# The up product of an MLP as seven half-size block products per unit

## The chip, the cores and the metric

One core of a Trainium2 chip runs two transformer blocks in float32 as one program. The metric is the device time in microseconds; less is better. TensorE (PE) multiplies into PSUM banks, VectorE (DVE) and ScalarE (ACT) prepare operands and take results, GpSimd (POOL) and SyncE (SP) issue transfers.

## The reference, cut to what matters

The first block (gated mixing, a recurrent branch, a mixture of experts) and the attention part of the second are the same in both kernels. Changed is the MLP at the end: x is 512 x 1024, w_ff1 1024 x 4096 and w_ff2 4096 x 1024, all float32.

```python
def rms_norm(x, g):
    xf = x.astype(jnp.float32)
    y = xf * lax.rsqrt(jnp.mean(xf * xf, axis=-1, keepdims=True) + EPS)
    return (y * g.astype(jnp.float32)).astype(x.dtype)
...
        h2 = rms_norm(x, norm_mlp[layer])
        x = x + jnp.square(jax.nn.relu(h2 @ w_ff1[layer])) @ w_ff2[layer]
    return rms_norm(x, norm_final)
```

## The kernel before

Every large float32 product is made of three fp32r products. An operand is split in two: ACT copies it to fp32r (the high part), DVE subtracts that from the original (the low part), and PE multiplies high by high, high by low and low by high into one bank. The activations h2, transposed to features by tokens (8 tiles of 128 features, 512 tokens), lie in `act_hi` and `act_lo`. The norm's scale is applied when results are added to `x`, so the row squares (`mlp_squares`, ACT) may be late.

The hidden width 4096 is worked in two halves, and each half is an up product followed by a down product. **An up product** has 4 units of 512 hidden columns; a unit has two chunks of 512 input rows, and a chunk four tiles of 12 matmuls, 128 weight columns by 512 tokens. Chunks alternate between the pairs `w_hi`/`w_lo` 0 and 1. SP loads chunk c into `w_stage[c % 2]` (1 MB) once chunk c - 2 has its low part; ACT may write chunk c's high part once PE has finished chunk c - 2; so a load has about two chunks of time. ACT takes each bank with a ReLU, DVE squares it into `hidden`.

**A down product** is already seven half-size block products (parts 0 to 6) of a 512 x 2048 by 2048 x 1024 product: each part has two steps of 24 matmuls, 512 columns wide, 14 steps in all. Part n's A operand (a quarter of `hidden` or a sum of quarters, `sum_three`, `sum_two`, `sum_one`, `sum_four`) goes to `part_hi`/`part_lo`, a step's weight block to `w_hi`/`w_lo`; `step_stage` names the buffer of each step. Sums of weight blocks are not made by DVE: ACT negates a loaded block (`negate`), and POOL issues transfers that add another block to it in SBUF (`add_block`, number k of 1 to 5 for each of kc = 0, 1, in that program order; each waits for the one before it on the same block column). Steps 4 and 5 need two adds, steps 8 and 9 the third (`b_one[1]`, `b_far`), steps 6 and 7 the fourth (`w_stage`), steps 12 and 13 the fifth. In the kernel before, `b_sum` is negated behind unit 1 of a half and `b_one[1]` and `b_far` behind its unit 2.

Nothing plans the order: each engine runs its own list as written (`two_blocks` has one section per engine), and semaphores tie them together. An instruction that waits holds all that stands behind it on its engine. The lists that matter are SP's at L820 to L850, POOL's at L1011 to L1030, ACT's at L1605 to L1705, DVE's at L2600 to L2705 and PE's at L3500 to L3536. The pieces that repeat (the low part on DVE, an adding transfer on POOL):

```python
    def rest(dst, src, hi):
        return dve.tensor_tensor(dst, src, hi.bitcast(F32), ALU.subtract)
...
    def add_block(h, kc, k, dst, block):
        pool.wait_ge(b_added[kc], loaded(h, "added", k - 1))
        pool.dma_start(dst[:, :, :], block, accum_op=ALU.add).then_inc(b_added[kc], 16)
```

## Time and profile before

| | us |
|---|---|
| median of 3 runs | 1690.91 |
| lowest and highest | 1690.90, 1691.43 |
| the profiled execution | 1689.05 |
| its span, first to last instruction | 1687.4 |
| up product, second half | 87.25 |
| a down product | 76.2 |

The profile comes from one execution. PE is busy for 99% of the span, but the busy time of matmuls overlaps, so times of stages are read from starts. A row of a timeline gives start and duration and, in brackets, how long the engine was idle before it and what released it.

### The profile page before, as it was taken

To read this page: it belongs to the slowest core of one execution; us is meant where nothing else is said; L and a number is where in the kernel's file an instruction comes from. 1 tells how busy PE (TensorE), PEld (TensorE's weight loads), DVE (VectorE), ACT (ScalarE), POOL (GpSimd) and SP (SyncE) were. 2 spreads that over 40 slices of the span, in tenths; PEclk is the share of its full clock that TensorE was granted. 3 is DMA by queue.
4 is the path that set the end of the run, shared out by engine and by line. 5 is a ranking of instruction groups with operands and counts; after the bars stand their busy time and mean duration, and the time that the engine had idled before them with its cause. 6 is when DMAs were issued, how large, how long until landed. Compare 5 with 4: busy or idle time off the path is not lost.

```text
span 1687.4 us, 23046 instructions
## 1 busy us (share of the span) xinstructions
PE 1672.0 (99%) x9378; PEld 1217.1 (72%) x9378; DVE 896.4 (53%) x1217; ACT 618.6 (37%) x744; POOL 112.8 (7%) x168
## 2 busy tenths in 40 slices
PE   9999999999999999999999999999999999999998
PEld 7888888865454535454588877788888888888886
DVE  6425438452343334324668755567675544773487
ACT  6334433321111101111366633344642245652565
POOL 4000000000000000000011012210000001100100
PEclk9999999999999999999999999999999999999999
DMA  7332222948999999999541332124352358756974
GB/s 274 100 99 75 75 75 101 354 189 342 429 428 428 428 429 429 428 429 428 204 153 53 100 100 75 51 76 132 107 188 100 107 181 195 157 149 221 200 157 128
DMA packets 90703, 353.29 MB, mean 209 GB/s; under 512 B 7856, under 2 KB 7872, under 8 KB 78208
## 3 DMA queue, kind: packets, MB, share of 16 engines
q1 hardware_dynamic: 78288, 325.95, 50.4%
q0 software_dynamic: 12336, 26.23, 7.8%
q8 instruction: 56, 0.92, 0.2%
q14 instruction: 23, 0.19, 0.0%
HBM read 345.87 MB, written 6.29 MB: 209 GB/s over the span
## 4 chain that ended last, share of the span: by engine, by line
PE 97%; DMA 1%; DVE 1%; ACT 0%; issue 0%; POOL 0%; DVEq 0%; POOLq 0%; ACTq 0%
PE bank L2764 51%; PE bank L3117 12%; PE bank L3522 9%; PE bank L3130 7%; PE bank L3025 4%; PE bank L3065 3%; PE bank L3297 2%; PE bank L2789 2%; PE bank L2810 1%; DMA ring<-in_w 1%; PE bank L3327 1%; PE bank L3350 1%; PE bank L3397 1%; PE bank L3222 1%; PE bank L3430 0%; PE bank L3436 0%
## 5 line engine op out<-in xcount | busy, mean ns | idle before, releaser
L2764 PE MATMUL bank<-act_hi,w_hi 128*128 128x512 f32 x992 | 390.0, 393 | 0.0
L2764 PE MATMUL bank<-act_hi,w_lo 128*128 128x512 f32 x992 | 386.2, 389 | 0.0
L2764 PE MATMUL bank<-act_lo,w_hi 128*128 128x512 f32 x992 | 386.2, 389 | 0.0
L1754 DVE TENSOR_TENSOR w_lo<-w_stage,w_hi 128x2048 fp32r<-128x2048 f32 x79 | 181.1, 2293 | 208.9 <-ACT w_hi L1044 208.8
L1044 ACT ACTIVATE w_hi<-w_stage 128x2048 fp32r<-128x2048 f32 x79 | 151.4, 1917 | 242.0 <-PE bank L2764 223.7
L3117 PE MATMUL bank<-ring,xgT 128*64 128x512 f32 x992 | 216.1, 592 | 1.8 <-ACT xgT L1266 1.4
L2764 PEld LDWEIGHTS bank<-act_hi,w_hi 128*128 128x128 f32 x992 | 186.2, 188 | 40.8 <-issue 2.9
L2764 PEld LDWEIGHTS bank<-act_hi,w_lo 128*128 128x128 f32 x992 | 186.2, 188 | 39.1
L2764 PEld LDWEIGHTS bank<-act_lo,w_hi 128*128 128x128 f32 x992 | 186.3, 188 | 37.7
L3117 PEld LDWEIGHTS bank<-ring,xgT 128*64 128x64 f32 x992 | 71.0, 137 | 143.0 <-issue 139.5
L3130 PE MATMUL bank<-ring,gatedT 128*64 128x512 f32 x512 | 113.4, 595 | 3.1 <-DMA ring<-in_w 2.3
L1294 ACT ACTIVATE y_hi_sb<-bank,slot_tables 128x512 fp32r<-128x512 f32 x32 | 22.0, 687 | 224.7 <-PE bank L3130 223.4
L2143 DVE TENSOR_TENSOR gated<-gated,bank 128x512 f32<-128x512 f32 x16 | 11.0, 688 | 161.7 <-PE bank L3117 161.7
L3130 PEld LDWEIGHTS bank<-ring,gatedT 128*64 128x64 f32 x512 | 35.8, 137 | 72.4 <-issue 68.7
L3522 PE MATMUL bank<-w_hi,part_hi 128*128 128x512 f32 x224 | 87.1, 389 | 0.0
L3522 PE MATMUL bank<-w_lo,part_hi 128*128 128x512 f32 x224 | 87.1, 389 | 0.0
L3522 PE MATMUL bank<-w_hi,part_lo 128*128 128x512 f32 x224 | 87.1, 389 | 0.0
L2118 DVE TENSOR_TENSOR x_tm<-x_tm,bank 128x512 f32<-128x512 f32 x128 | 78.5, 681 | 0.3 <-PE bank L3065 0.3
L2764 PE MATMUL bank<-w_hi,act_hi 128*128 128x512 f32 x160 | 62.8, 393 | 0.0
L2764 PE MATMUL bank<-w_hi,act_lo 128*128 128x512 f32 x160 | 62.3, 390 | 0.0
L2764 PE MATMUL bank<-w_lo,act_hi 128*128 128x512 f32 x160 | 62.3, 389 | 0.0
L2159 DVE SCALAR_TENSOR_TENSOR y_lo_sb<-bank,slot_tables,y_hi_sb 128x512 fp32r<-128x512 f32 x32 | 23.2, 749 | 73.4 <-ACT y_hi_sb L1294 73.1
(490 smaller groups left out, 2366.6 us busy)
## 6 DMA issues: line engine op xcount, KB each, us to landing
ring<-in_w SPq DMA_DIRECT2D x94, 2048.0 KB, 16.8
w_stage<-in_w_in SPq DMA_DIRECT2D x42, 1024.0 KB, 5.1
w_stage<-in_w_ff SPq DMA_DIRECT2D x24, 1024.0 KB, 5.6
b_sum<-in_w_ff POOLq DMA_DIRECT2D x12, 1024.0 KB, 12.7
w_stage<-in_w_out SPq DMA_DIRECT2D x8, 1024.0 KB, 5.0
b_one<-in_w_ff SPq DMA_DIRECT2D x6, 1024.0 KB, 7.7
branch_gates<-gate_out POOLq DMA_DIRECT2D x16, 256.0 KB, 2.5
w_stage<-in_w_proj_gla SPq DMA_DIRECT2D x4, 1024.0 KB, 9.9
```

What stands on the lines that cost most here:

```text
L1044: act.activation(w_hi[s][:, 0:ktiles, :], w_stage[s][:, 0:ktiles, :], ACT.Copy)\
L1754: dve.tensor_tensor(w_lo[s][:, 0:ktiles, :], w_stage[s][:, 0:ktiles, :], w_hi[s][:, 0:ktiles, :].bitcast(F32), ALU.subtract).then_inc(w_lo ...
L2118: dve.tensor_tensor(xt, xt, bank[:, :], ALU.add).then_inc(moe_added, 1)
L2159: dve.scalar_tensor_tensor(y_lo_sb[:, half], gb[1 + b][:, :], slot_gate[:, col(i)], y_hi_sb[:, half].bitcast(F32), ALU.mult, ALU.subtract)\
L2764: ins = pe.matmul(banks[j][:, :], left, right, start=(kc == 0 and k == 0 and n_pass == 0), stop=(kc == g.chunks - 1 and k == g.ktiles - 1 ...
L2789: return pe.transpose(dst, src, ident[0:rows, 0:rows])
L3025: return pe.matmul(bank[:, (k % 2) * 2 * P:(k % 2 + 1) * 2 * P], part[:, t, k * P:(k + 1) * P], sel[:, t, :], start=start, stop=(part is x ...
L3065: ins = pe.matmul(bank[:, :], selT[:, t * P:(t + 1) * P], part[:, half], start=(part is y_hi_sb), stop=(part is y_lo_sb))
L3117: ins = pe.matmul(dst[mine, :], xgT[:, 4 * kh + k, slots], up_weights(2 * w + kh, q, k, ahead), start=(kh == 0 and k == 0), stop=(kh == 1 ...
L3130: return pe.matmul(gb[1 + nh][mine, :], gatedT[:, k, mine], ring[4 + k // 2][:, 4 * q + 2 * (k % 2) + nh, :], start=(k == 0), stop=(k == 3 ...
L3297: ins = pe.matmul(v_bank[n][j][:, :], left[:, k0 + k, cols], right[:, k, :], start=(part_first[n] and k == 0 and n_pass == 0), stop=(k == ...
L3522: ins = pe.matmul(part_bank[n][j][:, :], left[:, ka, cols], right[:, k, :], start=(part_first[n] and kc == 0 and k == 0 and n_pass == 0), ...
```

## The change

Unit 0 of the up product stays as it was. Units 1 to 7 (`BLOCKED` = 7) become one run ahead of both down products. A unit's product, 512 weight columns by 1024 rows by 512 tokens, is cut in halves in all three, and made of seven products of half-size blocks: a product has 24 matmuls with 128 weight columns as the stationary operand and 256 tokens as the moving one, two groups of 128 hidden columns into the two halves of one bank.

The token side needs four sums T1 to T4 of quarters of h2, made once; for that ACT copies each transposed tile twice, to `raw_T` in plain float32 and to `act_hi`. The weight side needs sums W1 to W4 for each unit, on DVE. The weight blocks' high and low parts go to three slots of half size, so that ACT may write product m's slot when product m - 3 is done. Loads of a unit are now one of 1 MB and two of 0.5 MB with rows of 1 KB. Banks are shared by several products: ACT copies partial sums out, DVE adds, ACT does ReLU and square. All 32 tiles of `hidden` are kept (`F + 0` on, 64 KB a partition), so buffers of the down product move, and `b_one[1]` (now in the space of `act_lo`) and `b_far` are loaded at the end of unit 7 and negated behind step 2's high part. The second down product's first loads, first operands and `b_sum` adds are issued during the first one.

The core of the diff (the order of steps 3 to 13 inside a down product is otherwise as before):

```diff
+    g_up = Gemm(g_out2, 1, 2, "act")
+    BLOCKED = FF // 512 - 1
+    g_blk = Gemm(g_up, BLOCKED, PARTS, "act", tiles=3)
+    sums_added = g_blk.out["dve"]
+    g_blk.out["dve"] += 3 * BLOCKED
+    g_down = []
+    for h in range(HALVES):
+        g_down.append(Gemm(g_down[-1] if h else g_blk, 2, PARTS, "dve", tiles=PARTS))
...
+        slot_page = (41, 45, 37)
+        slot_hi = [at(f"slot_hi{s}", page, [P, 4, 256], F32R) for s, page in enumerate(slot_page)]
+        slot_lo = [at(f"slot_lo{s}", page + 2, [P, 4, 256], F32R) for s, page in enumerate(slot_page)]
+        w11, w21 = w_stage[0][:, :, 0:256], w_stage[0][:, :, 256:512]
+        w12, w22 = w_stage[1][:, :, 0:256], w_stage[1][:, :, 256:512]
+        w_sum = [at(f"w_sum{s}", 8 + 2 * s, [P, 4, 256]) for s in range(2)]
...
+            for u in range(1, BLOCKED + 1):
+                if u == 1:
+                    sp.wait_ge(w_lo_done, split_count(g_up.chunk0))
+                else:
+                    sp.wait_ge(hid_summed, w_summed(u - 1, W3))
+                load_rows(w_stage[0][:, :, :], 0, 512 * u, 512, w_loaded[0])
+                if u == 1:
+                    sp.wait_ge(w_lo_done, split_count(g_up.chunk0 + 1))
+                else:
+                    sp.wait_ge(hid_summed, w_summed(u - 1, W4))
+                load_rows(w12, 1, 512 * u, 256, w_loaded[1])
+                if u > 1:
+                    sp.wait_ge(w_lo_done, blk_split(u - 1, 6))
+                load_rows(w22, 1, 512 * u + 256, 256, far_loaded)
...
+            sp.wait_ge(hid_summed, w_summed(BLOCKED, W3))
+            sp.dma_start(w_stage[0][:, :, :], weight_block(0, 0, 0, 0)).then_inc(w_loaded[0], 16)
+            sp.wait_ge(w_lo_done, blk_split(BLOCKED, 5))
+            sp.wait_ge(pe_tiles, products_done(BLOCKED, 3))
+            sp.dma_start(b_one[1][:, :, :], weight_block(0, 0, 1, 0)).then_inc(b_one_in[1], 16)
+            sp.dma_start(b_far[:, :, :], weight_block(0, 0, 1, 1)).then_inc(b_one_in[0], 16)
+            sp.wait_ge(w_lo_done, blk_split(BLOCKED, 6))
+            sp.dma_start(w_stage[1][:, :, :], weight_block(0, 0, 0, 1)).then_inc(w_loaded[1], 16)
+            for h in range(HALVES):
                 for kc in range(2):
                     sp.wait_ge(w_lo_done, step(h, kc))
...
-                act.activation(act_hi[:, 4 * b:4 * b + 4, t * P:(t + 1) * P],
-                               mb[t][:, :].rearrange("p (k t) -> p k t", k=4), ACT.Copy).then_inc(n_hi, 1)
+                turned = mb[t][:, :].rearrange("p (k t) -> p k t", k=4)
+                act.activation(raw_T[:, 4 * b:4 * b + 4, t * P:(t + 1) * P], turned, ACT.Copy).then_inc(raw_copied, 1)
+                act.activation(act_hi[:, 4 * b:4 * b + 4, t * P:(t + 1) * P], turned, ACT.Copy).then_inc(n_hi, 1)
...
+            def slot_high(u, n):
+                m = product(u, n)
+                act.wait_ge(pe_tiles, 4 * (g_blk.chunk0 + max(m - 2, -1)))
+                if n == 0:
+                    act.wait_ge(w_loaded[0], 16 * (g_up.chunk1 // 2 + u))
+                elif n == 1:
+                    act.wait_ge(w_loaded[1], 16 * (g_up.chunk1 // 2 + u))
+                elif n == 6:
+                    act.wait_ge(far_loaded, 48 + 16 * u)
+                else:
+                    act.wait_ge(hid_summed, w_summed(u, {2: W2, 3: W1, 4: W3, 5: W4}[n]))
+                source = (w11, w12, w_sum[1][:, :, :], w_sum[0][:, :, :], w_sum[0][:, :, :], w_sum[1][:, :, :], w22)[n]
+                act.activation(slot_hi[m % 3][:, :, :], source, ACT.Copy).then_inc(w_hi_done, 1)
...
+            split_hi(g_up.chunk0 + 1, 1)
+            t_high(T2)
+            t_high(T3)
+            for t in range(NT):
+                mlp_squares(t)
+            own.settle()
+            act.sem_inc(n_sd, NT)
+            slot_high(1, 0)
+            slot_high(1, 1)
+            for j in range(4):
+                act.wait_ge(pe_tiles, (g_up.chunk0 + 1) * 4 + j + 1)
+                if j >= 2:
+                    act.wait_ge(hid_sq, j - 1)
+                act.activation(relu_t[j % 2][:, :], gb[j][:, :], ACT.Relu).then_inc(out_act, 1)
+                act.wait_ge(out_act, g_up.tile0 + 4 + j + 1)
+                act.activation(hidden[:, j, :], relu_t[j % 2][:, :], ACT.Square).then_inc(hid_sq, 1)
...
+            for u in range(1, BLOCKED + 1):
+                slot_high(u, 2)
+                if u == 1:
+                    t_high(T1)
+                copy_first(u)
+                slot_high(u, 3)
+                if u > 1:
+                    relu_sum(u - 1, ADD_12, blk_both)
+                slot_high(u, 4)
+                if u == 1:
+                    t_high(T4)
+                else:
+                    square(u - 1, 0, 1, blk_both)
+                    relu_last(u - 1)
+                copy_both(u)
+                if u > 1:
+                    square(u - 1, 1, 0, blk_last)
+                slot_high(u, 5)
+                copy_fifth(u)
+                slot_high(u, 6)
+                relu_sum(u, ADD_11, blk_first)
+                if u < BLOCKED:
+                    slot_high(u + 1, 0)
+                else:
+                    part_split_hi(0, 0)
+                square(u, 0, 0, blk_first)
+                if u < BLOCKED:
+                    slot_high(u + 1, 1)
+                else:
+                    step_split_hi(0, 0)
+                relu_sum(u, ADD_22, blk_fifth)
+                square(u, 1, 1, blk_fifth)
+                if u in (3, 4):
+                    negate_sums(0, u - 3)
+            step_split_hi(0, 1)
+            relu_sum(BLOCKED, ADD_12, blk_both)
+            square(BLOCKED, 0, 1, blk_both)
+            relu_last(BLOCKED)
+            square(BLOCKED, 1, 0, blk_last)
+            part_split_hi(0, 1)
+            for h in range(HALVES):
                 step_split_hi(h, 2)
+                for kc, block in enumerate((b_one[1], b_far)):
+                    act.wait_ge(b_one_in[1 - kc], loaded(h, "one", 1))
+                    negate(block, block)
...
+                    elif h + 1 < HALVES:
+                        negate_sums(h + 1, n - 3)
...
+            def t_add(n):
+                if n > T1:
+                    dve.wait_ge(hid_summed, V_SUMS + n - 1)
+                left, right = {T1: (r12, r11), T2: (r22, t_sum[0][:, :, :]), T3: (r22, r12),
+                               T4: (r21, t_sum[1][:, :, :])}[n]
+                dve.tensor_tensor(t_sum[n - 1][:, :, :], left, right, ALU.subtract).then_inc(hid_summed, 1)
...
+            split_lo(g_up.chunk0 + 1, 1)
+            dve.wait_ge(raw_copied, NH + 2 * NT)
+            for n in (T1, T2, T3, T4):
+                t_add(n)
+            t_low(T2, 1)
+            t_low(T3, 2)
+            slot_low(1, 0)
+            slot_low(1, 1)
+            for u in range(1, BLOCKED + 1):
+                first, second, third = blk_banks(u)
+                w_add(u, W1)
+                w_add(u, W2)
+                slot_low(u, 2)
+                if u == 1:
+                    t_low(T1, 3)
+                slot_low(u, 3)
+                w_add(u, W3)
+                w_add(u, W4)
+                slot_low(u, 4)
+                if u == 1:
+                    t_low(T4, 4)
+                if u in THIRD_SUMS:
+                    sum_three(THIRD_SUMS.index(u))
+                blk_add(u, ADD_11, 1, CP_FIRST, blk_first, second)
+                slot_low(u, 5)
+                slot_low(u, 6)
+                if u == BLOCKED:
+                    part_split_lo(0, 0)
+                blk_add(u, ADD_22, 4, CP_FIFTH, blk_fifth, first)
+                if u < BLOCKED:
+                    slot_low(u + 1, 0)
+                else:
+                    step_split_lo(0, 0)
+                blk_add(u, ADD_12, 5, CP_BOTH, blk_both, third)
+                if u < BLOCKED:
+                    slot_low(u + 1, 1)
+            step_split_lo(0, 1)
+            part_split_lo(0, 1)
...
+            def block_product(u, n):
+                m = product(u, n)
+                pe.wait_ge(w_lo_done, blk_split(u, n))
+                if n == 0:
+                    if u == 1:
+                        pe.wait_ge(raw_copied, NH + 2 * NT)
+                    else:
+                        pe.wait_ge(hid_sq, hid_count(max(u - 1, 1)))
+                elif n == 1 and u > 2:
+                    pe.wait_ge(out_dve, blk_added(u - 2, ADD_11))
+                elif n == 2:
+                    pe.wait_ge(out_act, blk_copied(u, CP_FIRST))
+                    pe.wait_ge(n_lo, T_LOWS + 1)
+                elif n == 3:
+                    pe.wait_ge(n_lo, T_LOWS + 3)
+                    if u > 2:
+                        pe.wait_ge(out_dve, blk_added(u - 2, ADD_12))
+                elif n == 4:
+                    pe.wait_ge(out_act, blk_copied(u, CP_BOTH))
+                elif n == 5:
+                    pe.wait_ge(out_act, blk_copied(u, CP_FIFTH))
+                elif n == 6:
+                    pe.wait_ge(n_lo, T_LOWS + 4)
+                    pe.wait_ge(out_dve, blk_added(u, ADD_22))
+                near, far = slice(0, 256), slice(256, 512)
+                b_hi, b_lo = ((act_hi[:, 0:4, near], act_lo[:, 0:4, near]), (act_hi[:, 4:8, near], act_lo[:, 4:8, near]),
+                              (t_hi[1], t_lo[1]), (t_hi[0], t_lo[0]), (t_hi[2], t_lo[2]),
+                              (act_hi[:, 4:8, far], act_lo[:, 4:8, far]), (t_hi[3], t_lo[3]))[n]
+                bank = blk_banks(u)[(0, 1, 0, 2, 0, 2, 0)[n]]
+                hi, lo = slot_hi[m % 3], slot_lo[m % 3]
+                for f in range(2):
+                    cols = slice(f * P, (f + 1) * P)
+                    for k in range(4):
+                        for n_pass, (left, right) in enumerate(((hi, b_hi), (hi, b_lo), (lo, b_hi))):
+                            ins = pe.matmul(bank[:, 256 * f:256 * f + 256], left[:, k, cols], right[:, k, :],
+                                            start=(n in (0, 1, 3) and f == 0 and k == 0 and n_pass == 0),
+                                            stop=(k == 3 and n_pass == 2), skip_group_check=True)
+                ins.then_inc(pe_tiles, 4)
```

## Rows read from the trace of the kernel before

**Rows 1.** The page's part 4: the chain that ended last, by engine.

```profile
PE 97%; DMA 1%; DVE 1%; ACT 0%; issue 0%; POOL 0%; DVEq 0%; POOLq 0%; ACTq 0%
```

**Rows 2.** Stretches: us, busy PE, PEld, DVE, ACT, POOL (count), clock, DMA share, GB/s.

```profile
1376.40:1441.68 65.28, 65.28 (x290) 54.07 (x289) 26.20 (x20) 27.23 (x23) 7.86 (x6) 1.00 0.84 212
1441.68:1517.84 76.16, 76.16 (x338) 62.84 (x336) 61.46 (x39) 45.40 (x25) 5.13 (x4) 1.00 0.62 144
```

**Rows 3.** Chain that ended last, in order of time: start, us, what.

```profile
1441.68 76.16 PE bank L3522 x336
1517.84 87.25 PE bank L2764 x384
1605.09 76.17 PE bank L3522 x336
```

**Rows 4.** Instructions of ACT around unit 0: start, us, what, [idle before].

```profile
1360.07 0.60 ACT L1608 ACTIVATE act_hi<-bank 128x512 fp32r<-128x512 f32 x1 [2.60 <-PE bank L2789]
1360.57 1.91 ACT L1044 ACTIVATE w_hi<-w_stage 128x2048 fp32r<-128x2048 f32 x1
1362.37 1.05 ACT L1624 ACTIVATE mlp_squared<-x_tm 128x1024 f32<-128x1024 f32 x1
...
1367.21 1.92 ACT L1044 ACTIVATE w_hi<-w_stage 128x2048 fp32r<-128x2048 f32 x1 [0.18 <-ACT mlp_squared L1624]
...
1376.44 0.60 ACT L1634 ACTIVATE relu_t<-bank 128x512 f32<-128x512 f32 x1 [2.12 <-PE bank L2764]
```

**Rows 5.** Instructions of DVE, same stretch.

```profile
1362.50 2.29 DVE L1754 TENSOR_TENSOR w_lo<-w_stage,w_hi 128x2048 fp32r<-128x2048 f32 x1 [1.11 <-ACT w_hi L1044]
```

**Rows 6.** Instructions of PE in one expert gather.

```profile
404.20 0.64 PE L3025 MATMUL bank<-sel,xn_lo 128*128 128x256 f32 x4
...
410.92 0.64 PE L3025 MATMUL bank<-sel,xn_lo 128*128 128x256 f32 x4
```

**Rows 7.** Groups by line and shape, PE: count, busy us, mean ns, idle before.

```profile
L3025 PE MATMUL bank<-sel,xn_hi 128*128 128x256 f32 x256 | 41.8, 288 | 1.2 <-DVE sel L2111 1.2
...
L3415 PE MATMUL bank<-gv_tm,gkend_tm 128*128 128x256 f32 x24 | 5.3, 379 | 0.0
```

**Rows 8.** Groups by line and shape, ACT, from 840 us on.

```profile
L1646 ACT ACTIVATE part_hi<-hidden 128x2048 fp32r<-128x2048 f32 x12 | 22.8, 1904 | 0.2
L1634 ACT ACTIVATE relu_t<-bank 128x512 f32<-128x512 f32 x32 | 19.1, 596 | 52.0 <-PE bank L2764 44.9 <-DVE hidden L2634 7.1
...
L1409 ACT ACTIVATE low_hi<-low_f 128x1024 fp32r<-128x1024 f32 x1 | 1.1, 1062 | 0.0
```

**Rows 9.** Groups by line and shape, DVE, from 840 us on.

```profile
L1769 DVE TENSOR_TENSOR part_lo<-hidden,part_hi 128x2048 fp32r<-128x2048 f32 x12 | 27.4, 2285 | 0.0
...
L2341 DVE TENSOR_TENSOR gv_tm<-gv_tm,bank 128x512 f32<-128x512 f32 x6 | 4.0, 684 | 2.5 <-PE bank L3297 2.5
...
L1769 DVE TENSOR_TENSOR v_part<-v_raw,v_part 128x1024 fp32r<-128x1024 f32 x3 | 3.7, 1219 | 0.0
```

**Rows 10.** DMA queues and issues, 1413 to 1436 us: share of 16 engines; us to landing.

```profile
q0 software_dynamic: 1800, 3.56, 83.8%
q1 hardware_dynamic: 1024, 2.06, 26.7%
...
w_stage<-in_w_ff SPq DMA_DIRECT2D x3, 1024.0 KB, 12.3
```

**Rows 11.** Tile w_stage, issues of POOL from 1458 to 1464: us to landing.

```profile
DMA to landing us min/median/max: 8.8/10.0/11.3
```

**Rows 12.** Instructions of POOL: start, us, issue, [idle before <-releaser].

```profile
1415.01 1.30 POOL L1014 DMA_DIRECT2D b_sum<-in_w_ff  x1 [9.20 <-DMA b_sum<-in_w_ff]
1421.08 1.30 POOL L1014 DMA_DIRECT2D b_sum<-in_w_ff  x1 [4.76 <-DMA b_sum<-in_w_ff]
```

**Rows 13.** DMA issues, 1381 to 1383 us: KB each, us to landing.

```profile
w_stage<-in_w_ff SPq DMA_DIRECT2D x1, 1024.0 KB, 5.5
...
b_far<-in_w_ff SPq DMA_DIRECT2D x1, 1024.0 KB, 9.8
```

402 lines of the change are left out of this document (239 added, 163 removed).

## The prediction

> **What bounds the kernel now.** I read four views, widest first. The chain that ended last is 97% TensorE [rows 1]. The stretches by stage show PE busy for all of each MLP stretch at a granted clock of 1.00, its upper level, 2.4 GHz, with DVE and ACT well below it [rows 2]: no stage waits for a helper, so each matmul removed is time removed, as long as the helpers keep up. The chain in order of time gives the pitch: a down product is 336 matmuls in 76.16 us, 226.7 ns each; the second half's up product 384 in 87.25 us, 227.2 ns [rows 3]. "Mean ns of one" (389) is no pitch, since matmuls overlap. Unit 0 ends where the last ReLU begins, about 1376.4 [rows 4], so units 1 to 7 take 65.3 us (1376.4 to 1441.68) and 87.25 us: 152.5 us. The last question is how much slack ACT, DVE and the two DMA queues have; the remaining groups are for that.
>
> **The matmuls: -11.4 us.** 7 units x 7 products x 24 = 1176 matmuls of 256 columns replace 672 of 512. The expert gather is made of fp32r matmuls of that size [rows 7], with a weight load each as here: 14 groups of four start between 404.20 and 410.92 [rows 6], so 6.72/56 = 0.120 us. 1176 x 0.120 = 141.1 us, against 152.5. A product lasts D = 2.88 us, a unit 20.16. PE's waits between products are given nothing: the 14 steps of a down product show none in 226.7 ns.
>
> By the Trainium skill (TensorE: Matmul & The Clock Gate, Back-to-back issue gap) the gap is N/2.4 + 2.5 ns, that is 109.2 ns for 256 and 215.8 ns for 512 columns; by it this term would be 145.0 - 128.4 = 16.6 us, and my result 5.2 us lower. This trace shows 120.0 and 226.7, about 11 ns above it at both sizes, and the measurement decides.
>
> **A unit in the steady state: 0.** ACT per unit: seven splits of 1024 columns (1.06), and eleven operations of 512 (0.60) [rows 8], 14.0 us; DVE: seven lows and four sums of 1024 (1.22) and three adds (0.68) [rows 9], 15.5 us; both under 20.2. With unit start at 0, in program order: the sums W1, W2 end at 1.8, split 2 is ready at 4.1 (due at 2D = 5.8), split 3 at 5.7 (8.6), split 4 at 9.3 (11.5), split 5 at 12.3 (14.4), split 6 at 14.3 (17.3), the next unit's split 0 at 16.8 (20.2), split 1 at 19.6 (23.0). The bank copies come one product ahead. The thinnest spare is 1.6 us, at split 2; the A sum of 2.3 us in units 5 and 7 falls behind split 4 and fits.
>
> **The start: +1.8 us.** ACT now copies each transposed tile twice. The last arrives at 1360.07; the second chunk's split starts 0.5 later than its 1360.57 [rows 4], and w_lo, at 1362.50 before [rows 5], ends about 1365.3. PE needs it at 1376.4 - 48 x 0.2267 = 1365.5: hidden, spare 0.2. Then DVE makes T1 to T4, each waiting for the one before (ends 1366.4, 1367.7, 1368.9, 1370.2); ACT splits T2 and T3 (to 1370.0), does the four row squares (1362.37 to 1367.21 before, 4.8 us [rows 4]) to 1374.8, and the first weight block by 1375.8; its low is done at 1377.1. Due 1376.4: +0.7. ACT next does unit 0's four ReLU and square pairs, which wait for each other (1.15 each, to 1381.2), split 2, T1's high and the copy of product 0's bank: 1383.7, due 1377.1 + 2D = 1382.8: +0.9. The same for product 4: +0.2.
>
> **Weight loads beside the accumulating loads: +6.0 us.** While adds are in flight a 1 MB stage load lands after 12.3 us (q0 83.8%, q1 26.7%) [rows 10]; alone it takes 5.5 [rows 13]. Before, a load had the time of two chunks, 2 x 10.9 us, and that was enough. Now the next unit's first block is issued behind W3, at 7.0, and due on ACT at 17.9. The adds: b_sum's two negations end units 3 and 4, so kc1's first add, kc0's second and kc1's second follow one another in unit 5, from 1.5. An add alone lands after 8.8, one issued 3.6 us behind it after 11.3 [rows 11], so they queue, 6.1 us each (6.07 between the releases of [rows 12]): q0 is busy to about 25, and the queue of unit 6's loads with it. First block 19.3, low 21.7, due 20.2: +1.5. The 0.5 MB block behind it has 1 KB rows, which no row of the trace shows: between 5.2 us (by bytes) and 10.3 (by the packet count); I take 6, since q0 drains meanwhile: landed 25.5, low 27.9, due 24.6: +3.3, or +2.1 at the short end; I take +2.7. Product 2 then needs W1, W2, high and low behind that low, 4.7 us less D: +1.8. The bounds are 0 (no slowing) and 7.5.
>
> **From up to down: +3.8 us.** In unit 7 the low of the first A part stands ahead of the add that product 6 waits for. Part high (1.90) ends at 15.4 on ACT, part low (2.29) at 17.7, the add at 18.3, due 17.3: +1.0. SP issues b_one, b_far and w_stage[1] together at about 13.2; three such loads land one behind the other (5.5, ..., 9.8 [rows 13]), so w_stage[1] is in at 23.9, its low at 28.15, and step 1 is due at 21.2 + 5.44 = 26.65: +1.5. That high holds ACT's queue: the last two squares, part 1's high (30.0) and low (32.2), the scale and step 2's low on DVE (34.9) follow; due 33.7: +1.3.
>
> **The down products: +11.3 us.** Their matmuls are the same, 76.16 each [rows 3]. New is that b_one and b_far are negated behind step 2's high, no longer in the up product, and POOL issues their add (its third) ahead of the fourth, into w_stage, which step 6 needs. With N the end of the first negation: third adds land at N + 9.1 and N + 15.2, the fourth issued at N + 9.5 lands behind both at N + 21.3; high and low make N + 25.6. First half: N = 33.6, ready 59.2, due 34.9 + 4 x 5.44 = 56.7: +2.5; step 7 likewise +0.7. Second half, from its own start: b_sum's negations stand behind the highs of steps 10 and 12, so their adds run until about 10; step 2's w_stage load, issued at -1.2 when step 0's low is done, lands at 10.7, not at 4.3; low 15.0, due 10.9: +4.1. N = 14.5, ready 40.1, due 36.7: +3.4; step 7 +0.6. Together 3.2 + 8.1.
>
> **Nothing:** the squares go from DVE to ACT; part 0's bank waits end with products long done; the tail behind the last matmul (1605.09 + 76.17 to the span's 1687.4 [rows 3], 6.1 us) is untouched.
>
> **Sum.** -11.4 + 1.8 + 6.0 + 3.8 + 11.3 = +11.5 us. Profiled: span 1687.4 + 11.5 = 1698.9, its run 1689.05 + 11.5 = 1700.6; the median stands 1.86 above the profiled run, so 1702.4.
>
> **Rivals.**
> F, faster: the adds and loads share the engines without queueing. The third add, then the fourth, each take the 8.8 us of a lone add: N + 22.6, which is ready at 56.2 and 31.8, ahead of 56.7 and 32.6. Place: the w_stage add for step 6; it decides where that add lands before N + 18.8 in the first half. Unit 6's blocks then land as a lone load does (5.5 [rows 13]), in time. Left: -11.4 + 1.8 + 3.8 = -5.8, 1685.1. For it: DMA is idle in parts of the down stretch (share 0.62 [rows 2]). Against: 11.3 behind 8.8 [rows 11]. 0.15.
> S, same: only loads beside adds come in time (the q1 share is larger when fewer loads stand in it), while adds queue: -11.4 + 1.8 + 3.8 + 3.2 + 2.8 = +0.2, 1691.1. 0.20.
> W, worse: the spare of 1.6 us is used up by PE's two or three waits a product and by semaphore delays, 0.15 us for each of 49 products: 7.4 on top, 1709.8. Against: the gather keeps 0.120 across its waits. 0.14.
> X, the change doesn't do what it says: a 256-column matmul at 5.34/24 = 0.22 us, as in the other group of that size [rows 7], would take 262 us in all, some 1800. That group's operands are plain fp32, these are fp32r. 0.02.
> Forecast 0.49.
>
> **Numbers.** 1702.4. The range leaves out X, most of F and the far side of W: 1686 to 1711. What a measurement of this kernel can tell from no change is 0.2%, 3.4 us. Faster: F less its slow part, 0.14. Same: S, and the edges of F and the forecast, 0.22. Slower: 0.64.
>
> **What would show it.** Products at 2.88 us between the starts of their first matmuls; idle PE ahead of unit 1 (0.7) and product 2 (0.9), ahead of the first three products of unit 6 (6), of unit 7's product 6 (1.0), of steps 1 and 2 in the first half and of step 2 in the second (4), and of step 6 in both (2.5, 3.4), the last with ACT released by a DMA of w_stage. If steps 6 start without idle time the sum falls by 7 us and S or F is right; a PE stall in every unit is W.

## The result and the profile after

The changed kernel takes 1707.51 us (median of 4, 1706.39 to 1709.54), the kernel before, on the same chip, 1690.91 (1690.76 to 1691.43): a ratio of 1.0099, 95% interval 1.0081 to 1.0116. It is 16.6 us slower. The forecast was 1702.4.

The profiled execution of after took 1706.39 us, its span 1704.5. PE ends 17.1 us later than before. The chain of the page, which was 97% PE and 1% DMA [rows 1], is now 87% PE, and more of it is waiting ("issue" is time in which the engine waited for nothing that the profile shows):

```profile
PE 87%; issue 5%; DMA 4%; DVE 2%; ACT 1%; POOL 0%; SPq 0%; DVEq 0%; ACTq 0%; POOLq 0%
```

The matmuls did what they were to do. The first row to read is the stretch from product 4 of unit 1 to the end of unit 5, between two stalls, in the view by stages (columns: window, its length, busy time and count of PE, weight loads, DVE, ACT, POOL, then granted clock, DMA share, GB/s):

```profile
1391.50:1480.80 89.30, 89.25 (x744) 89.28 (x744) 67.43 (x62) 57.97 (x78) 5.33 (x4) 1.00 0.60 168
```

744 narrow matmuls in 89.3 us are 0.1200 us each, through 31 products and all their waits. So the gain of 11.4 us is there. The loss stands in PE's timeline, in the rows with idle time ahead of them (start, duration, engine, line, operation; in brackets the idle time and who ended it). These are, in order: two at the start, three in unit 6, product 6 of unit 7, steps 1, 2, 6 and 11 of the first half, steps 2 and 6 of the second:

```profile
1378.75 0.39 PE L3819 MATMUL bank<-act_hi,slot_hi 128*128 128x256 f32 x1 [0.60 <-DVE slot_lo L1973]
1385.45 0.36 PE L3819 MATMUL bank<-t_hi,slot_hi 128*128 128x256 f32 x1 [0.68 <-DVE slot_lo L1973]
...
1483.61 0.39 PE L3819 MATMUL bank<-act_hi,slot_hi 128*128 128x256 f32 x1 [2.56 <-DVE slot_lo L1973]
...
1488.96 0.39 PE L3819 MATMUL bank<-act_hi,slot_hi 128*128 128x256 f32 x1 [0.72 <-DVE slot_lo L1973]
1493.77 0.39 PE L3819 MATMUL bank<-t_hi,slot_hi 128*128 128x256 f32 x1 [1.68 <-DVE slot_lo L1973]
...
1526.92 0.35 PE L3819 MATMUL bank<-t_hi,slot_hi 128*128 128x256 f32 x1 [1.22 <-DVE blk_fifth L2877]
...
1537.33 0.50 PE L3846 MATMUL bank<-down_hi,part_hi 128*128 128x512 f32 x1 [1.84 <-DVE down_lo L1973]
...
1543.98 0.47 PE L3846 MATMUL bank<-down_hi,part_hi 128*128 128x512 f32 x1 [0.91 <-issue]
...
1566.97 0.47 PE L3846 MATMUL bank<-down_hi,part_hi 128*128 128x512 f32 x1 [0.95 <-DVE down_lo L1973]
...
1600.78 0.79 PE L3846 MATMUL bank<-down_hi,part_hi 128*128 128x512 f32 x1 [6.32 <-DVE down_lo L1973]
...
1631.26 0.47 PE L3846 MATMUL bank<-down_hi,part_hi 128*128 128x512 f32 x1 [1.51 <-issue]
...
1654.53 0.47 PE L3846 MATMUL bank<-down_hi,part_hi 128*128 128x512 f32 x1 [1.20 <-issue]
```

The bracket counts from a matmul's modelled end. What a stall costs is start to start, less one pitch, and that is some 0.15 more in each row: 0.75, 0.84 (and 0.27 at product 4), 2.71, 0.87, 1.83, 1.38, 1.99, 1.07, 1.11, 6.48, 1.66, 1.36. I use these numbers from here on. They sum to 22.3 us.

DVE is named because its low comes last, but DVE had waited for ACT, and ACT for a load. ACT's timeline at the same places (unit 6's first two blocks, step 1, step 6, the negation ahead of step 11, step 2 of the second half):

```profile
1481.24 1.06 ACT L1753 ACTIVATE slot_hi<-w_stage 128x1024 fp32r<-128x1024 f32 x1 [6.72 <-DMA w_stage<-in_w_ff]
...
1486.60 1.06 ACT L1753 ACTIVATE slot_hi<-w_stage 128x1024 fp32r<-128x1024 f32 x1 [3.78 <-DMA w_stage<-in_w_ff]
...
1533.04 1.92 ACT L1820 ACTIVATE down_hi<-w_stage 128x2048 fp32r<-128x2048 f32 x1 [4.93 <-DMA w_stage<-in_w_ff]
...
1562.58 1.92 ACT L1820 ACTIVATE down_hi<-w_stage 128x2048 fp32r<-128x2048 f32 x1 [3.62 <-DMA w_stage<-in_w_ff]
...
1594.69 1.91 ACT L1824 ACTIVATE b_sum<-b_sum 128x2048 f32<-128x2048 f32 x1 [9.10 <-DMA b_sum<-in_w_ff]
1596.51 1.89 ACT L1820 ACTIVATE down_hi<-b_one 128x2048 fp32r<-128x2048 f32 x1
...
1626.91 1.92 ACT L1820 ACTIVATE down_hi<-w_stage 128x2048 fp32r<-128x2048 f32 x1 [4.22 <-DMA w_stage<-in_w_ff]
```

So 18.0 of the 22.3 us are late transfers or follow from them: all but the start (1.86), product 6 of unit 7 (1.38) and step 2 of the first half (1.07), which is the queue that step 1's late high leaves on ACT. The transfers of 1577, ahead of the largest stall (issue, size, median us to landing):

```profile
b_sum<-in_w_ff POOLq DMA_DIRECT2D x1, 1024.0 KB, 13.5
b_one<-in_w_ff SPq DMA_DIRECT2D x1, 1024.0 KB, 14.9
b_sum<-in_w_ff SPq DMA_DIRECT2D x1, 1024.0 KB, 17.2
```

A lone load took 5.5 [rows 13]. Only the b_one block of these is needed by step 11; it landed at 1592.0, and ACT took it at 1596.5, behind the negation of the next half's b_sum block.

Behind the two longest stalls PE runs at half its clock, for a while. By stages, in and behind those stretches (a count also takes in matmuls that started before the window):

```profile
1485.00:1487.00 2.00, 2.00 (x12) 2.00 (x11) 0.00 (x0) 0.41 (x1) 0.00 (x0) 0.50 0.81 280
...
1489.00:1491.00 2.00, 2.00 (x17) 2.00 (x18) 1.97 (x2) 0.00 (x0) 0.00 (x0) 1.00 0.00 0
```
```profile
1602.00:1603.00 1.00, 1.00 (x3) 0.79 (x3) 1.00 (x2) 1.00 (x1) 0.00 (x0) 0.50 1.13 209
...
1605.00:1606.00 1.00, 1.00 (x6) 0.80 (x5) 1.00 (x2) 0.00 (x0) 1.00 (x2) 1.00 1.05 408
```

The clock column is 0.50, the lower level, 1.2 GHz, and PE, though busy, starts a wide matmul every 0.43 us (1602.22, 1602.65, 1603.08) where it otherwise starts one every 0.227. Unit 6's product 0 takes 4.36 us from its first to its last start instead of 2.76: 1.6 lost; step 11 about 1.6. A third such stretch lies far ahead of the changed code. At 815 to 820 the clock column shows 0.66 after and 1.00 before, though PE's wait ahead of it is as long in both, 2.03 us after and 2.26 before:

```profile
815.39 7.07 PE L3413 MATMUL bank<-ring,gatedT 128*64 128x512 f32 x24 [2.03 <-DMA ring<-in_w]
...
815.00:820.00 5.00, 4.61 (x14) 1.77 (x16) 1.47 (x6) 0.00 (x0) 0.00 (x0) 0.66 0.96 360
```
```profile
815.00:820.00 5.00, 4.46 (x22) 1.92 (x24) 1.38 (x5) 0.68 (x1) 0.00 (x0) 1.00 0.95 359
```

It costs 1.7 us and belongs to the execution, not to the change: the kernel before with only the adding transfers cut (below) falls to half speed there too, behind a wait of 2.10.

The account of the profiled run: -11.4 matmuls, +22.3 idle, +3.2 half-speed clock behind the stalls, +0.9 (each first matmul after a stall takes some 0.1 longer), +1.7 at 815: 16.7, of 17.1 seen between the two profiles.

### The profile page after: what moved, and what is told of

Read it like the earlier page. It is cut to its first block, busy times and chain, and to the rows that moved or that the text cites. A ratio compares the mean times of both kernels' runs of the same rounds, so it can differ in the third digit from the quotient of the medians.

```text
span 1704.5 us, 24246 instructions
## 1 busy us (share of the span) xinstructions
PE 1668.9 (98%) x9882; PEld 1235.1 (72%) x9882; DVE 957.7 (56%) x1277; ACT 675.6 (40%) x844; POOL 112.0 (7%) x168
## 3 DMA queue, kind: packets, MB, share of 16 engines
q1 hardware_dynamic: 81984, 325.95, 49.4%
## 4 chain that ended last, share of the span: by engine, by line
PE 87%; issue 5%; DMA 4%; DVE 2%; ACT 1%; POOL 0%; SPq 0%; DVEq 0%; ACTq 0%; POOLq 0%
PE bank L3047 40%; PE bank L3400 12%; PE bank L3413 7%; PE bank L3846 6%; PE bank L3819 4%; PE bank L3308 4%; PE bank L3348 3%; PE bank L3580 2%; PE bank L3072 2%; DMA b_sum<-in_w_ff 2%; PE bank L3093 1%; DMA ring<-in_w 1%; PE bank L3610 1%; PE bank L3633 1%; PE bank L3680 1%
## 5 line engine op out<-in xcount | busy, mean ns | idle before, releaser
L3047 PE MATMUL bank<-act_hi,w_hi 128*128 128x512 f32 x768 | 303.1, 395 | 0.0
L3047 PE MATMUL bank<-act_hi,w_lo 128*128 128x512 f32 x768 | 299.5, 390 | 0.0
L3047 PE MATMUL bank<-act_lo,w_hi 128*128 128x512 f32 x768 | 299.4, 390 | 0.0
L3047 PEld LDWEIGHTS bank<-act_hi,w_hi 128*128 128x128 f32 x768 | 144.2, 188 | 32.2 <-issue 2.9
L3846 PE MATMUL bank<-down_hi,part_hi 128*128 128x512 f32 x224 | 88.6, 396 | 12.7 <-DVE down_lo L1973 9.1
L3846 PE MATMUL bank<-down_hi,part_lo 128*128 128x512 f32 x224 | 87.8, 392 | 0.0
L3846 PE MATMUL bank<-down_lo,part_hi 128*128 128x512 f32 x224 | 87.8, 392 | 0.0
L3819 PE MATMUL bank<-act_hi,slot_hi 128*128 128x256 f32 x224 | 64.6, 288 | 3.9 <-DVE slot_lo L1973 3.9
L3819 PE MATMUL bank<-act_lo,slot_hi 128*128 128x256 f32 x224 | 64.2, 287 | 0.0
L3819 PE MATMUL bank<-act_hi,slot_lo 128*128 128x256 f32 x224 | 64.1, 286 | 0.0
```

The costliest lines, as they stand in the source:

```text
L3047: ins = pe.matmul(banks[j][:, :], left, right, start=(kc == 0 and k == 0 and n_pass == 0), stop=(kc == g.chunks - 1 and k == g.ktiles - 1 ...
L3819: ins = pe.matmul(bank[:, 256 * f:256 * f + 256], left[:, k, cols], right[:, k, :], start=(n in (0, 1, 3) and f == 0 and k == 0 and n_pass ...
L3846: ins = pe.matmul(part_bank[h][n][j][:, :], left[:, ka, cols], right[:, k, :], start=(part_first[n] and kc == 0 and k == 0 and n_pass == 0 ...
```

## The experiments

Idle times are PE's, start to start less a pitch, as above. The median of the kernel before was 1691.1 to 1691.6 in the groups of runs below.

### The adding transfers cut

```diff
-                pool.dma_start(dst[:, :, :], block, accum_op=ALU.add).then_inc(b_added[kc], 16)
+                pool.dma_start(dst[:, 0:1, 0:16], block[:, 0:1, 0:16], accum_op=ALU.add).then_inc(b_added[kc], 16)
```

In the changed kernel (this leaves out nearly all of each addition):

> The changed kernel, with POOL's adding transfers cut to one partition block and 16 columns each: this leaves out nearly all of the addition of the weight blocks (the sums B22-B11 and the like), so the products are made of the wrong sums, but every instruction, wait and matmul stays. Theory (the 1 MB adding transfers crowd the loads and the later adds): the stalls ahead of unit 6 (2.7 + 0.9 + 1.8), of step 6 in both halves (1.1, 1.4), of step 11 in the first half (6.5) and of step 2 in the second (1.7) all go, 14.3 us by the idle stretches of PE, and with them 3 to 4 us of half-speed clock behind two of them: 1707.5 - 14.3 - 3.5 = 1689.7, down to 1686. The stalls at the start (1.9) and at steps 1 and 2 of the first half stay. Rival (the order of the work on ACT and DVE makes the stalls, and the transfers would be in time without it): PE's idle stretches at these places stay within 0.5 us each, 1705 to 1708. Between them: the first block of unit 6 in time, the second not; about 1695.

Measured: 1687.12 us (ratio 0.9979, interval 0.9970 to 0.9989). The five places named have no idle time left, the start keeps 1.90, product 6 of unit 7 keeps 1.38 and step 1 of the first half 2.06. The 1.07 ahead of step 2, which was to stay, is gone as well: in this profile the clock is at its lower level from 1528.0 to 1531.4, behind the 2.06, so PE comes to step 2 some 1.7 us later. The control, the kernel before with the same cut:

> The kernel before with the same cut of the adding transfers (the same addition left out). It is the control for the other: theory, the adds cost nothing in the kernel before, because a load had two chunks' time there: 1690.9, within 1 us. Rival: the adds cost matmul time also there, by sharing the memory with PE's operands: then it is 3 us or more faster, and what the other kernel gains is partly that.

Measured: 1691.27 (1.0004, 0.9994 to 1.0013). The adds cost the kernel before nothing and the changed one some 20 us. The DMA share of the two parts of the down stretch says how full the engines are. After, then after with the cut:

```profile
1560.00:1605.00 45.00, 37.73 (x159) 30.49 (x158) 30.20 (x19) 25.93 (x14) 4.29 (x4) 0.92 1.02 265
1605.00:1640.00 35.00, 33.49 (x148) 27.37 (x147) 25.35 (x17) 22.45 (x13) 6.14 (x6) 1.00 0.94 213
```
```profile
1560.00:1605.00 45.00, 45.00 (x200) 37.24 (x200) 33.93 (x22) 28.95 (x16) 4.38 (x5) 1.00 0.58 192
1605.00:1640.00 35.00, 35.00 (x156) 29.00 (x155) 33.28 (x20) 27.04 (x15) 4.33 (x5) 1.00 0.22 62
```

The share adds up the times of all packets, and so can pass 1. After, the engines are busy nearly all of the time, at only 213 to 265 GB/s. The page's part on DMA queues tells why (packets, MB, share of 16 engines' span). After:

```profile
q1 hardware_dynamic: 81984, 325.95, 49.4%
q0 software_dynamic: 12336, 26.23, 7.7%
```

With the cut:

```profile
q0 software_dynamic: 4656, 5.43, 1.2%
```

The 20.8 MB of adds that were cut took 7.7% of 1704.5 less 1.2% of 1682.9, 111 us of all sixteen engines: 5.3 us for each MB. A load's MB took 2.6 (49.4% of 1704.5, over 326).

### The adds of the first half spread

```diff
-                if u in (3, 4):
-                    negate_sums(0, u - 3)
+                if u in (2, 3):
+                    negate_sums(0, u - 2)
...
                 for kc in range(2):
+                    if h == 0:
+                        pool.wait_ge(hid_summed, w_summed(5 + kc, W2))
                     add_block(h, kc, 2, b_sum[h][kc], weight_block(h, 0, 0, kc))
```

> The changed kernel with the adds of the first half spread out: the negations of b_sum's two halves at the ends of units 2 and 3, not 3 and 4, and POOL's second add of each held until units 5 and 6, so that about one adding transfer is in flight in a unit in place of three in a row. Theory (three adds in a row delay unit 6's loads): the 5.4 us idle ahead of unit 6's first three products goes and with it the 1.7 us that PE lost at half-speed clock behind it: 1707.5 - 7.1 = 1700.4. Rival 1: the loads of unit 6 are late by one add alone (12.3 us beside any add): the stall falls to about 1.5, in each of the units with an add: 1703 to 1707. Rival 2: the late adds now hold the down product's first adds: idle at step 10 or 11 grows, no gain.

Measured: 1700.33 (1.0058, 1.0041 to 1.0075), 7.2 less. POOL's timeline, the adds now one in a unit:

```profile
1441.92 1.30 POOL L1121 DMA_DIRECT2D b_sum<-in_w_ff  x1 [18.76 <-ACT b_sum L1826]
1462.90 1.30 POOL L1121 DMA_DIRECT2D b_sum<-in_w_ff  x1 [19.68 <-DVE w_sum L2859]
1482.90 1.30 POOL L1121 DMA_DIRECT2D b_sum<-in_w_ff  x1 [18.70 <-DVE w_sum L2859]
```

Unit 6 has no idle time, and its half-speed stretch is gone too. So it was three adds in a row, and not an add as such: the load beside the one at 1462.90 landed after 7.8 us, in time. Steps 6 and 11 keep their idle time (1.61 and 6.80).

### Step 11: issued earlier, loads moved, negation moved

Three edits at the 6.5 us. First, SP's b_sum loads ahead of step 8's wait:

```diff
-                sp.wait_ge(w_lo_done, step(h, 8))
-                sp.dma_start(b_one[1][:, :, :], weight_block(h, 1, 1, 1)).then_inc(b_one_in[1], 16)
                 if more:
                     sp.wait_ge(part_low, V_PARTS + PARTS * h + 5)
                     for kc in range(2):
                         sp.dma_start(b_sum[1][kc][:, :, :], weight_block(h + 1, 0, 1, kc)).then_inc(b_sum_in[kc], 16)
+                sp.wait_ge(w_lo_done, step(h, 8))
+                sp.dma_start(b_one[1][:, :, :], weight_block(h, 1, 1, 1)).then_inc(b_one_in[1], 16)
+                if more:
```

> The changed kernel with SP's loads for b_sum of the next half issued ahead of the wait for step 8's low and of b_one's load behind it, in each half. Theory: the 6.5 us idle ahead of step 11 in the first half comes from ACT, which waits 9.1 us with the negation of b_sum for a load that lands 17 us after its issue; issued about 5 us earlier it is there 5 us earlier or more, and the idle falls to 1.5 or less, with the 1.5 us of half-speed clock: 1707.5 - 6.5 = 1701. Rival: the load lands at the same time, since it is queued behind the adds and not late in its issue: 1707.5. It may also push b_one's load later: then a new idle stretch of 1 to 3 us at steps 9 or 10 shows it.

Measured: 1707.86, idle 7.40. The rival's time held, its reason only in part: the b_sum load, issued 2.3 us earlier, did land earlier, at 1592.9 for 1594.7. But the b_one block that step 11 needs, now behind the b_sum loads, landed at 1598.3 for 1592.0, and so took longer after its issue than the 14.9 shown above:

```profile
b_sum<-in_w_ff SPq DMA_DIRECT2D x1, 1024.0 KB, 20.0
b_sum<-in_w_ff POOLq DMA_DIRECT2D x1, 1024.0 KB, 13.6
b_one<-in_w_ff SPq DMA_DIRECT2D x1, 1024.0 KB, 20.2
```

Second, the loads that nobody needs yet go last:

```diff
-                if more:
-                    sp.wait_ge(w_lo_done, step(h, 6))
-                    sp.dma_start(w_stage[0][:, :, :], weight_block(h + 1, 0, 0, 0)).then_inc(w_loaded[0], 16)
...
-                if more:
-                    sp.wait_ge(w_lo_done, step(h, 7))
-                    sp.dma_start(w_stage[1][:, :, :], weight_block(h + 1, 0, 0, 1)).then_inc(w_loaded[1], 16)
...
                     sp.dma_start(b_far[:, :, :], weight_block(h + 1, 0, 1, 1)).then_inc(b_one_in[0], 16)
+                    sp.dma_start(w_stage[0][:, :, :], weight_block(h + 1, 0, 0, 0)).then_inc(w_loaded[0], 16)
+                    sp.dma_start(w_stage[1][:, :, :], weight_block(h + 1, 0, 0, 1)).then_inc(w_loaded[1], 16)
```

> The changed kernel with SP's two w_stage loads for the second half's steps 0 and 1 issued behind the b_far load (after step 10's low) in place of ahead of the first half's b_one and b_sum loads; they were issued at 1566.9 and 1571.9 and are not needed before 1608 and 1612. Theory (the 6.5 us ahead of step 11 is transfers queued behind transfers: two adds of 6.1 us and six loads of some 2.2 us each from 1566.6 on): two loads fewer in that queue make the b_one and b_sum loads land 4.3 us earlier, the idle time falls to about 2 and the half-speed clock behind it goes too: 1707.5 - 4.3 - 1.5 = 1701.7, as far as 1703.2 if the clock still falls. Rival: they are late for their own issue or by the adds alone: idle stays above 5 and the time within 1 us of 1707.5. The second half's steps 0 and 1 should stay without idle time.

Measured: 1706.98 (1.0096, 1.0079 to 1.0113). Idle ahead of step 11 fell from 6.48 to 3.42, and ahead of step 2 of the second half it rose from 1.66 to 4.57. Sum 7.99, where it had been 8.14: the loads that went last were worth 3.1 us ahead of step 11, and the gain was nil. Third, on ACT alone:

```diff
                     step_split_hi(h, 2 * n + 3)
+                    if n == 4 and h + 1 < HALVES:
+                        negate_sums(h + 1, 0)
                     part_split_hi(h, n + 2)
...
-                    elif h + 1 < HALVES:
-                        negate_sums(h + 1, n - 3)
+                    elif n == 4 and h + 1 < HALVES:
+                        negate_sums(h + 1, 1)
```

> The changed kernel with ACT's negation of the second half's first b_sum block behind step 11's high in place of ahead of it. Theory: ACT stands 9.1 us at that negation for a load that step 11 does not need, while the b_one block that it does need lands at 1592.0, 4.5 us before its high starts at 1596.5; with the negation behind it the idle time ahead of step 11 falls from 6.5 to 2.0: 1707.5 - 4.5 = 1703.0, and 1701.5 if the clock no longer falls to half. Rival: the second half's b_sum adds start later for it and its steps 2 to 6 lose the same: more than 1.7 idle ahead of step 2.

Measured: 1707.75. Idle 2.17 ahead of step 11, as worked out, and 3.84 ahead of step 2 of the second half, as the rival has it: 6.0 for 8.1, and yet no gain, since both stalls now have half-speed clock behind them. By stages, in the two stretches:

```profile
1600.00:1602.00 2.00, 2.00 (x6) 1.52 (x6) 2.00 (x2) 2.00 (x2) 0.00 (x0) 0.50 1.07 374
...
1633.00:1635.00 2.00, 2.00 (x6) 1.52 (x6) 1.75 (x2) 2.00 (x2) 0.23 (x1) 0.50 1.09 194
```

Each of these edits moved waiting from one stall to the next. From 1560 to 1640 the DMA share is 1.02 and 0.94, so there is hardly any free DMA time to move a transfer to.

### From up to down, and the order of POOL's adds

```diff
-            sp.wait_ge(w_lo_done, blk_split(BLOCKED, 5))
+            sp.wait_ge(w_lo_done, blk_split(BLOCKED, 6))
+            sp.dma_start(w_stage[1][:, :, :], weight_block(0, 0, 0, 1)).then_inc(w_loaded[1], 16)
             sp.wait_ge(pe_tiles, products_done(BLOCKED, 3))
             sp.dma_start(b_one[1][:, :, :], weight_block(0, 0, 1, 0)).then_inc(b_one_in[1], 16)
             sp.dma_start(b_far[:, :, :], weight_block(0, 0, 1, 1)).then_inc(b_one_in[0], 16)
...
+                blk_add(u, ADD_22, 4, CP_FIFTH, blk_fifth, first)
                 if u == BLOCKED:
                     part_split_lo(0, 0)
-                blk_add(u, ADD_22, 4, CP_FIFTH, blk_fifth, first)
```

> The changed kernel with two orders swapped at the end of unit 7: SP loads the block of w_stage[1] before those of b_one and b_far, and DVE makes the sum for the hidden quarter 22 before the low of the first A part. Theory: the 1.4 us idle ahead of product 6 of unit 7 is the low standing ahead of the sum on DVE, and goes; the 2.0 us ahead of step 1 is the w_stage[1] load landing 10.1 us after its issue behind the two others, and goes with a load of some 5.5 us; the 1.1 us ahead of step 2 is the queue that this late high leaves on ACT, and goes with it. 1707.5 - 4.4 = 1703.1. Rival: the loads of b_one and b_far, now behind it, make the two negations late, and the idle time goes over to step 2 or step 6 (over 1 us more there): 1705 to 1707.5.

Measured: 1704.90 (1.0084, 1.0067 to 1.0101), 2.6 less. The idle time ahead of product 6 and of step 1 went (1.38 and 1.99), that ahead of step 2 rose from 1.07 to 1.63: its own w_stage load, now behind b_one and b_far, took 8.3 us for 6.6. The rival had named these two loads and step 2, but through the negations, not through this load. The other order:

```diff
+                for kc in range(2):
+                    pool.wait_ge(b_negated, NEGATED * h + 5 + kc)
+                    add_block(h, kc, 3, w_stage[kc], weight_block(h, 1, 1, kc))
                 for kc in range(2):
                     pool.wait_ge(b_negated, NEGATED * h + 3 + kc)
-                    add_block(h, kc, 3, (b_one[1], b_far)[kc], weight_block(h, 1, 1, kc))
-                for kc in range(2):
-                    pool.wait_ge(b_negated, NEGATED * h + 5 + kc)
-                    add_block(h, kc, 4, w_stage[kc], weight_block(h, 1, 1, kc))
+                    add_block(h, kc, 4, (b_one[1], b_far)[kc], weight_block(h, 1, 1, kc))
```

> The changed kernel with POOL's adds into w_stage (for steps 6 and 7) ahead of those into b_one and b_far (for steps 8 and 9), in each half. Theory (step 6 is late because its add queues behind two others): the first w_stage add is issued when its negation ends, about 1550.2 in place of 1552.8, into an empty queue, lands after some 9 us near 1559 in place of 1562.6, and the 1.1 us idle ahead of step 6 in the first half and the 1.4 us in the second go: 1707.5 - 2.5 = 1705.0. Rival: the b_one adds, now last, make steps 8 and 9 late by as much: no gain, 1707.5. Since all adds are in flight at the same places otherwise, the 6.5 us ahead of step 11 should stay.

Measured: 1713.60, 6.1 more. Neither of the two: step 6 has no idle time left in either half, but steps 9 and 11 of the first have 2.03 and 10.49:

```profile
1584.45 0.50 PE L3846 MATMUL bank<-down_hi,part_hi 128*128 128x512 f32 x1 [1.87 <-DVE down_lo L1973]
...
1605.95 0.80 PE L3846 MATMUL bank<-down_hi,part_hi 128*128 128x512 f32 x1 [10.33 <-DVE down_lo L1973]
```

POOL's adds into b_one and b_far now start when the first w_stage add has landed, at 1559.3 and 1564.7 where they had started at 1543.0 and 1545.2, and push all that is behind: the b_sum load that ACT negates ahead of step 11 took 23.4 us. In the second half, where no further half's transfers follow, the same swap costs 1.59 at step 9 and gains 1.36 at step 6.

### The narrow matmul alone

The kernel before, units 1 to 7 with each tile's tokens in two runs of 256 (`toks`), eight products as before:

```diff
+                    for q in range(2):
+                        toks = slice(256 * q, 256 * q + 256)
...
+                                ins = pe.matmul(banks[j][:, toks], left, right,
```

> The kernel before with the up product of units 1 to 7 in matmuls of 256 columns in place of 512, the same eight products and the same work: 1344 narrow matmuls for 672 wide ones, every weight load twice. It prices the narrow matmul alone. Theory, by the pitch of the trace (0.120 us): 1344 x 0.120 = 161.3 in place of 152.5, 8.8 us more: 1699.8. Rival, by the Trainium skill (TensorE: Matmul & The Clock Gate, Back-to-back issue gap: 109.2 ns at 256 columns): 146.8, 5.8 us less: 1685.1.

Measured: 1700.22 (1.0047, 1.0030 to 1.0064), by the medians 8.7 above the kernel before in the same runs, for 8.8 forecast. The chain in order of time (start, us, what, count):

```profile
1378.97 69.11 PE bank L2763 x576
```

69.11/576 = 0.1200 us. By the 109.2 ns of the Trainium skill (TensorE: Matmul & The Clock Gate, Back-to-back issue gap) the narrow matmuls would take an estimated 146.8 us; at 0.1200 they take 161.3. The section gives this as the gap of an isolated matmul, and by it the wide ones too would be quicker than measured (145.0 us for 152.5), so by the page at both sizes this kernel would be 1.8 us slower than before. The rival above, 5.8 us faster, had set the page's narrow matmul against the measured wide one. The measurement decides, at both sizes. The eighth that seven products save is 19.1 us of 152.5, and narrow matmuls take back 7/8 of 8.8, or 7.7: 11.4 are left.

### The orders mended together

The spread adds, the order at the handover, the late loads and the late negation together, and three moves more (the core of each; two of the row squares go behind split 3 of unit 1 and two to its end):

```diff
+            sp.wait_ge(w_lo_done, step(0, 0))
+            sp.dma_start(w_stage[0][:, :, :], weight_block(0, 1, 0, 0)).then_inc(w_loaded[0], 16)
             sp.wait_ge(pe_tiles, products_done(BLOCKED, 3))
             sp.dma_start(b_one[1][:, :, :], weight_block(0, 0, 1, 0)).then_inc(b_one_in[1], 16)
...
+                    elif kc == 1:
+                        pool.wait_ge(w_loaded[0], loaded(h, "stage", 2))
...
-            for t in range(NT):
-                mlp_squares(t)
             slot_high(1, 0)
```

> The changed kernel with the orders of transfers mended together, nothing of the computation changed: the first half's b_sum adds spread over units 3 to 6; at the end of unit 7 SP loads w_stage[1], then w_stage[0] for step 2, then b_one and b_far, and DVE makes the sum for quarter 22 ahead of the first part's low; the second half's w_stage loads behind the b_far load and the negation of its first b_sum block behind step 11's high; POOL's last b_sum add of the second half held until the w_stage load for its step 2 has landed; the row squares moved from ahead of unit 1 into its gaps. By the idle stretches of PE: 7.1 less at unit 6 (measured alone: 7.2), 4.0 at the handover, 6 at step 11, 1.7 ahead of step 2 of the second half, 0.7 at the start, and 1.5 to 3 of half-speed clock: 1707.5 - 21.5 = 1686, down to 1684. Then the narrow block products do pay, by what is left of the 11.4 us. Rival (idle time moves on to the next place that waits for a transfer, since the queues are full in the down stretch): 5 us or more at other steps, 1691 or more.

Measured: 1690.65 (1.0002, 0.9993 to 1.0012): level with the kernel before. Idle: 0.89 ahead of step 2 of the first half, none at the start, at unit 6 and at step 11; but 6.05 ahead of step 2 of the second half and 1.74 ahead of its step 6. The start's idle time went entirely, 1.9 and not 0.7. Half theory, half rival. ACT at the one large stall:

```profile
1608.45 1.91 ACT L1823 ACTIVATE down_hi<-w_stage 128x2048 fp32r<-128x2048 f32 x1 [8.62 <-DMA w_stage<-in_w_ff]
```

This load took 13.5 us, beside the b_sum adds of 1584.0 and 1592.9, which are needed later than it is. So the last version holds both second adds for the load, and in the second half alone the w_stage adds go first:

```diff
-                    elif kc == 1:
+                    else:
                         pool.wait_ge(w_loaded[0], loaded(h, "stage", 2))
...
+                for n in ((3, 4), (4, 3))[h]:
```

> The kernel with the mended orders, with two more in its second half: both second b_sum adds held until the w_stage load for step 2 has landed, and the adds into w_stage ahead of those into b_one and b_far. What is left in that kernel is 0.9 idle ahead of step 2 of the first half, 6.05 ahead of step 2 of the second, where the w_stage load lands 13.5 after its issue beside two adds, and 1.7 ahead of its step 6. Theory: with one add less in flight the load lands after 8 to 9, the stall falls to about 1, and step 6 no longer waits behind b_one's add: 1690.7 - 5 - 1 = 1684.7, 0.4% under the kernel before. Rival: the adds' chain is full from there on, so what is gained at step 2 is lost again at steps 4 to 9 of the second half (idle there over 4): 1689 to 1691.

Measured: 1684.42 us (median of 5, 1683.43 to 1685.15; 0.9958, 0.9945 to 0.9972), 7.2 under the kernel before in the same runs and 23 under the change as it was made. The load takes 7.7, the longest stall is 0.93, and the clock column is 1.00 in the whole MLP:

```profile
1560.00:1605.00 45.00, 44.41 (x196) 36.45 (x196) 33.34 (x21) 27.97 (x15) 3.88 (x3) 1.00 1.02 290
1605.00:1640.00 35.00, 34.90 (x155) 28.54 (x154) 32.50 (x21) 28.09 (x16) 9.02 (x7) 1.00 1.06 210
```

The DMA engines are at least as full as after (1.02 and 1.06, for 1.02 and 0.94), and PE, at 44.41 of 45 and 34.90 of 35 us, hardly waits for them. Which of the two last moves gave how much was not run apart.

## Why the prediction was right or wrong

**Matmuls, right.** 0.1200 us in three traces. The rival of 0.15 us for each product's waits (W) is refuted by the 31 products without a gap, and so is X. W's time, 1709.8, lies near the measured one all the same, for another reason.

**Start, right:** 1.86 for 1.8, each of the three places within 0.1.

**Unit 6, right in mechanism, sum near:** 5.4 for 6.0. Its first block landed at 1481.2, and three adds in a row are the cause, as the spread adds show. The parts were not as given: 2.71, 0.87 and 1.83 for 1.5, 2.7 and 1.8. They also change between executions: two of the kernels above whose edits touch only step 11 (b_sum loads issued earlier, negation late) show 2.54, 3.01, 0.55 and 2.48, 3.03, 0.43 at unit 6, with the half-speed stretch behind the second block and not the first. Their sums are 6.1 and 5.9.

**From up to down, right:** 4.4 for 3.8, at the three places named.

**The third and fourth adds, the term oversized.** Step 6: 1.11 for 2.5, and 1.36 for 3.4; step 7, no idle time for 0.7 and 0.6; step 2 of the second half 1.66 for 4.1. The adds did queue. But I gave the fourth 11.8 us (issued at N + 9.5, landed at N + 21.3). It was issued at 1552.79:

```profile
1552.79 1.28 POOL L1121 DMA_DIRECT2D w_stage<-in_w_ff  x1 [6.28 <-DMA b_one<-in_w_ff]
```

It landed at 1562.58, where ACT's high starts: 9.8 us, and with the negation's end at 1542.7, N + 19.9. The spacing of 6.1 us for one add behind another was too wide here: these four landed at 1552.2, 1557.4, 1562.6 and 1567.6, 5.0 to 5.2 apart. Step 2 of the second half was sized by a load landing 11.9 us after its issue; it took 9.1.

**The down products' list of what is new, wrong.** The step said that only b_one's and b_far's adds were new. It followed their own readers (step 6, step 7) and not what else waits in the same queues. The next half's transfers are new in the first down product as well, and the sum gave them no price there. From 1566.6 to 1594.7, beside the fifth adds and the two b_one loads that the kernel before has there too, stand five loads for the next half: w_stage twice (5.7 and 16.3 us), b_sum twice (17.2 and 19.3) and b_far (12.0). ACT stood 9.1 us at the first b_sum block's negation, and the high of step 11 stood behind that. 6.5 us, in no term and no rival. The experiments say what it is made of: without the two w_stage loads it is 3.4, with the negation behind the high 2.2, without the adds nothing. The two new adds themselves had landed by 1557.4. What they did was to hold the fourth (above, released by b_one's landing), and with it step 6's high on ACT and the negations behind it that the fifth adds wait for.

**The clock, missing.** 3.2 us at half speed behind the two longest stalls. No term had it, and neither had the rivals.

The two errors went opposite ways: the terms for steps 2, 6 and 7 were 7.2 us too high (11.3 for 4.1), steps 11 and the clock 9.7 too low. So it is partly luck that the time stands 5.1 us from the forecast and inside the range. The mechanism (loads queue behind adds) was right, and the place of its largest cost was not foreseen.

**The rivals F and S** are refuted at the places they named. F had the w_stage add landed before N + 18.8 and step 6 without idle time; it landed at N + 19.9, and step 6 had 1.11. With that add first in its queue (the swapped adds) it took 8.4 us and the idle time went, so it had queued. Both had the loads beside adds in time; unit 6 had 5.4 us idle, which goes with the adds cut or spread. The cut kernel's 1687.1 is near F's 1685.1, since F is the kernel in which the adds delay nothing.

**The measured margin.** The profile of before has no half-speed stretch ahead of the MLP, and the profile of after has the one at 815. But the forecast stands on before's median, 1.86 us above that profile. Of the 48 executions of before in the groups of the experiments 37 have a mean clock of 0.998 and a median of 1691.4 us, the other 11 have 0.999 and 1689.8. So most executions of before probably have such a stretch too: the 1.7 us belong to the 17.1 between the two profiles, and need not be in the 16.6 between the medians. No clock is on record for the four runs of before in that comparison, so this stays an estimate.
